# The second block of the channel mixer: all seven-product sets, behind the first down product

## The chip, the cores and the metric

The kernel runs on one NeuronCore of a Trainium2 chip. The metric is the device time of one execution in microseconds. The time before is a median of 2115.37 us over three runs (2115.2 to 2117.08).

## The reference, cut to what matters

Two layers of a diffusion backbone on 640 tokens (512 latent and 128 context tokens). Each layer mixes tokens (retention and neighbourhood attention), adds the result to the residual, and ends with a channel mixer. The change lies in the channel mixer alone:

```python
D_MODEL = 1024; DEPTH = 2
D_FF = -(-8 * D_MODEL // (3 * 256)) * 256          # 2816

def swiglu(h, wg, wu, wd):
    return (jax.nn.silu(h @ wg) * (h @ wu)) @ wd

def block_tail(...):
    ...
    x = x + g1[:, None, :] * rmsnorm(mixed, n_post_mix)
    hf = modulate(rmsnorm(x, n_pre_ffn), sh2, sc2)
    return x + g2[:, None, :] * rmsnorm(swiglu(hf, w_ffn_gate, w_ffn_up, w_ffn_down), n_post_ffn)
```

## The kernel before, in words

**Numbers as two halves.** Every fp32 operand of a matmul is split into a high part (a copy to fp32r by ScalarE) and a low part (the difference, by VectorE). A product is three matmuls: high by high, high by low, low by high (`product`, L502 to L504; `linear`, L514 to L517). Weights come in slabs of 128x1024 fp32, 512 KB each, from `w_main` into the buffers `raw`; `wh` and `wl` hold their halves (ScalarE's and VectorE's `split`). SP issues the slabs in the order in which `main_slabs` lays them, each as soon as the last user of its buffer is done. The modulated tokens stand feature by feature in `hmh` and `hml` (8 chunks of 128 features, 640 tokens).

**The blocks.** The 2816 hidden features are 11 blocks of 256 (`FB`). A block needs two gate columns and two up columns of 128 features each, then silu(gate) times up gives its hidden activations (`hidh`, `hidl`), and its down product adds to the output of five token tiles (`down`, tiles of 128 tokens, 12 matmuls of 128x512 per tile).

**Plain columns.** A column is 8 chunks x 3 matmuls x 2 halves of 320 tokens, 48 matmuls of 128x320, in one of two PSUM buffers `unit`. Block 0 is all plain columns: `first_columns` computes three of them (up to two wait for the last token tile), and a `column` the fourth. Its second hidden column is gated on VectorE (L2298) once that fourth column is there, copied on ScalarE (L1599), and its low part taken on VectorE (`hid_ready`).

**Seven products.** A pair of columns (256x1024 weights by 1024x640 activations, taken as a 2x2 by a 2x2) is also computed with seven products instead of eight (`seven`; each product is 4 chunks x 3 = 12 matmuls of 128x320). That needs sums of the tokens, once per layer (`t1` to `t4`: `sum_of_tokens`, `last_sum_of_tokens`, low parts in `low_of_tokens`), and sums of the weights, once per pair (`pair_sums`: four operations of 128x512 into `e0w` or `e1w` and back into `raw`; then the halves of the two slabs and of the sums in three parts, `pair_high` on ScalarE, `pair_low` on VectorE). The products go round four PSUM banks (`place`). VectorE adds each to the others (`seven_add`, L2344), and TensorE waits for those additions (`seven_added`) before it writes a bank again: the sixth product waits for the first addition, the seventh for the second.

**The order around the change.** With `SEVEN = 2`, blocks 2 to 10 are sets of seven throughout, while block 1 is mixed: its two gate columns are plain and come right behind block 0's, then the down product of block 0, then one set of seven for block 1's up columns (`seven(0)`). So a layer has `SEVENS = 19` sets. From there on TensorE alternates two sets of seven for block b and the down product of block b-1. VectorE's order is written out by hand in `first_block`, `second_block` and `seven_block`, ScalarE's under the same names. GpSimd issues DMAs alone in this stretch (the copies of the tokens to `x_keep`, L1194).

## Time and profile before

| | |
|---|---|
| median of the runs | 2115.37 us |
| the profiled execution | 2116.27 us, its span on the core 2114.5 us |
| TensorE busy | 2092.1 us (99%), 13850 matmuls |
| VectorE busy | 1558.5 us (74%) |
| ScalarE busy | 937.1 us (44%) |
| GpSimd busy | 101.6 us (5%) |
| granted TensorE clock | 1.00 |

Busy time is the time in which an engine executes something. A matmul's row is longer than its share of the engine's time, as matmuls are pipelined: what one costs is the distance from its start to the next start. On VectorE and ScalarE too a row overlaps the next one by about 0.1 us. Times are microseconds from the span's start, and the idle time in brackets behind a row is the engine's wait just ahead of it and what ended it.

### The profile page before, as it was taken

To read this page: it belongs to the slowest core of one execution; us is meant where nothing else is said; L and a number is where in the kernel's file an instruction comes from. 1 tells how busy PE (TensorE), PEld (TensorE's weight loads), DVE (VectorE), ACT (ScalarE), POOL (GpSimd) and SP (SyncE) were. 2 spreads that over 40 slices of the span, in tenths; PEclk is the share of its full clock that TensorE was granted. 3 is DMA by queue.
4 is the path that set the end of the run, shared out by engine and by line. 5 is a ranking of instruction groups with operands and counts; after the bars stand their busy time and mean duration, and the time that the engine had idled before them with its cause. 6 is when DMAs were issued, how large, how long until landed. Compare 5 with 4: busy or idle time off the path is not lost.

```text
span 2114.5 us, 33751 instructions
## 1 busy us (share of the span) xinstructions
PE 2092.1 (99%) x13850; PEld 1993.0 (94%) x13850; DVE 1558.5 (74%) x2493; ACT 937.1 (44%) x1490; POOL 101.6 (5%) x195
## 2 busy tenths in 40 slices
PE   8999999999999999999999999999999999999998
PEld 6999999899989999999899999999999899999997
DVE  6688767777757887887877776755854688787786
ACT  6555432476335432333485554235743553233333
POOL 0000001110000000000000000011100000000000
PEclk9999999999999999999999999999999999999999
DMA  8333355324333222222433333532233312222223
GB/s 317 110 120 122 103 174 176 138 93 148 102 131 119 80 80 80 80 80 88 162 132 120 115 109 131 169 127 79 86 120 130 130 61 80 80 80 82 97 82 139
DMA packets 63241, 246.05 MB, mean 116 GB/s; under 512 B 7792, under 2 KB 8080, under 8 KB 60400
## 3 DMA queue, kind: packets, MB, share of 16 engines
q1 hardware_dynamic: 42480, 158.55, 21.6%
q0 software_dynamic: 20608, 85.35, 11.6%
q8 instruction: 110, 1.80, 0.3%
q14 instruction: 43, 0.35, 0.1%
HBM read 230.20 MB, written 13.66 MB: 115 GB/s over the span
## 4 chain that ended last, share of the span: by engine, by line
PE 93%; DVE 3%; ACT 2%; DMA 1%; issue 0%; DVEq 0%; POOL 0%; POOLq 0%
PE unit L502 11%; PE unit L503 11%; PE unit L504 11%; PE unit L514 10%; PE unit L517 10%; PE unit L515 10%; PE sc L502 4%; PE sc L503 4%; PE sc L504 4%; PE tp L502 4%; PE tp L503 4%; PE tp L504 4%; PE tp L862 1%; PE sc L838 1%; PE unit L889 1%; PE unit L888 1%
## 5 line engine op out<-in xcount | busy, mean ns | idle before, releaser
L1773 DVE TENSOR_TENSOR wl<-raw,wh 128x1024 fp32r<-128x1024 f32 x200 | 242.2, 1221 | 119.3 <-ACT wh L1224 117.3
L514 PE MATMUL unit<-hmh,wh 128*128 128x320 f32 x1056 | 318.5, 309 | 1.8 <-DVE vl L1783 1.5
L515 PE MATMUL unit<-hml,wh 128*128 128x320 f32 x1056 | 318.1, 309 | 0.0
L1224 ACT ACTIVATE wh<-raw 128x1024 fp32r<-128x1024 f32 x200 | 206.0, 1050 | 99.6 <-DMA raw<-w_main 99.5
L517 PE MATMUL unit<-hmh,wl 128*128 128x320 f32 x1056 | 240.6, 309 | 0.0
L1872 DVE CUSTOM_DVE_ANT_0 junk<-ada,csb,par 128x1024 f32<-128x1024 f32 x160 | 205.6, 1285 | 29.3 <-DMA ada<-w_ada 9.7
L514 PEld LDWEIGHTS unit<-hmh,wh 128*128 128x128 f32 x1056 | 198.3, 188 | 2.4 <-issue 2.4
L515 PEld LDWEIGHTS unit<-hml,wh 128*128 128x128 f32 x1056 | 198.3, 188 | 0.0
L502 PE MATMUL unit<-wh,hmh 128*128 128x256 f32 (+1 forms) x544 | 178.8, 329 | 0.3 <-DVE wl L1773 0.3
L503 PE MATMUL unit<-wl,hmh 128*128 128x256 f32 (+1 forms) x544 | 177.7, 327 | 0.0
L504 PE MATMUL unit<-wh,hml 128*128 128x256 f32 (+1 forms) x544 | 177.7, 327 | 0.0
L517 PEld LDWEIGHTS unit<-hmh,wl 128*128 128x128 f32 x1056 | 176.6, 188 | 0.0
L502 PE MATMUL unit<-wh,hidh 128*128 128x512 f32 x440 | 171.6, 390 | 0.0
L503 PE MATMUL unit<-wl,hidh 128*128 128x512 f32 x440 | 171.4, 390 | 0.0
L504 PE MATMUL unit<-wh,hidl 128*128 128x512 f32 x440 | 171.2, 389 | 0.0
L502 PE MATMUL unit<-hmh,wh 128*128 128x320 f32 (+2 forms) x384 | 123.5, 322 | 0.5 <-DVE hml L1783 0.5
L504 PE MATMUL unit<-hmh,wl 128*128 128x320 f32 (+2 forms) x384 | 118.7, 309 | 0.0
L503 PE MATMUL unit<-hml,wh 128*128 128x320 f32 (+2 forms) x384 | 118.6, 309 | 0.0
L502 PEld LDWEIGHTS unit<-wh,hmh 128*128 128x128 f32 x544 | 104.3, 192 | 9.1 <-issue 0.5
L504 PEld LDWEIGHTS unit<-wh,hml 128*128 128x128 f32 x544 | 104.3, 192 | 8.8
L503 PEld LDWEIGHTS unit<-wl,hmh 128*128 128x128 f32 x544 | 104.3, 192 | 8.5
L1620 ACT ACTIVATE wh<-raw 128x1024 fp32r<-128x1024 f32 x38 | 40.2, 1057 | 149.2 <-DVE e0w L2321 147.7
(472 smaller groups left out, 5431.6 us busy)
## 6 DMA issues: line engine op xcount, KB each, us to landing
raw<-w_main SPq DMA_DIRECT2D x276, 512.0 KB, 3.8
ada<-w_ada POOLq DMA_DIRECT2D x80, 512.0 KB, 4.5
first<-w_first SPq DMA_DIRECT2D x8, 1024.0 KB, 19.2
x<-x_keep POOLq DMA_DIRECT2D x3, 2560.0 KB, 11.1
bias<-biases POOLq DMA_DIRECT2D x32, 192.0 KB, 2.7
x_keep<-x POOLq DMA_DIRECT2D x10, 512.0 KB, 2.9
bias<-biases POOLq DMA_DIRECT2D x16, 256.0 KB, 4.1
gains<-g_rows POOLq DMA_DIRECT2D x4, 1024.0 KB, 6.1
```

The source lines that it names most:

```text
L502: pe.matmul(out, a[0], b[0], start=first, stop=False)
L503: pe.matmul(out, a[0], b[1], start=False, stop=False)
L504: return pe.matmul(out, a[1], b[0], start=False, stop=last)
L514: pe.matmul(u[:, h, 0:n], a[0], xs[h][0], start=f, stop=False)
L515: pe.matmul(u[:, h, 0:n], a[0], xs[h][1], start=False, stop=False)
L517: mm = pe.matmul(u[:, h, 0:n], a[1], xs[h][0], start=False, stop=z)
L838: pe.matmul(sc[hh][:, 0:n], (nqh, nql)[a][rows[hh], j * P:(j + 1) * P], (nkh, nkl)[b][rows[hh], first * P:first * P + n], start=t == 0, st ...
L862: mm = pe.transpose(tp[hh][:, to * P:(to + 1) * P], s[:, hh, n * P:(n + 1) * P], ident[:, :])
L1224: act.activation(wh[slot[i]][:, :], raw[slot[i]][:, :], ACT.Copy).then_inc(w_hi[slot[i]], 1)
L1620: act.activation(wh[slot[i + 1]][:, :], raw[slot[i + 1]][:, :], ACT.Copy).then_inc(w_hi[slot[i + 1]], 1)
L1773: dve.tensor_tensor(wl[slot[i]][:, :], raw[slot[i]][:, :], f32(wh[slot[i]][:, :]), ALU.subtract)\
L1872: a = dve.tensor_tensor_reduce(junk[:, :], ada[ada_slot[i]][:, :], csb[:, which, :], 1.0, par[:, l, B_ADA + chunk:B_ADA + chunk + 1], ALU. ...
```

## The change

All of block 1 becomes sets of seven (`SEVEN = 1`, 20 sets a layer), and they move behind the first down product, which now follows the fourth column at once. That down product takes its first two tiles chunk by chunk: the first half of both tiles waits for the first hidden column alone, the second half for the second. GpSimd computes the weight sums of block 1's two pairs. The slabs are laid in the new order. VectorE and ScalarE do block 0's and block 1's steps in a new hand-written order, and the sums of the third pair (block 2's gate columns) come inside the second set's additions.

```diff
-SEVEN, SIX = 2, 6
-SEVENS = 2 * (FB - SEVEN) + 1
+SEVEN, SIX = 1, 6
+SEVENS = 2 * (FB - SEVEN)
...
                 def down(b):
+                    weights = [slab(512)[1:] for _ in range(2)]
+                    units = []
+                    for k in range(2 if b == 0 else 0):
+                        pe.wait_ge(hid_ready, downs.value() * 2 + k + 1)
+                        for t in range(2):
+                            if k == 0:
+                                units.append(U.take())
+                                U.add()
+                            mm = down_part(units[t], b, t, k, weights, k == 0, k == 1)
+                            if k == 1:
+                                mm.then_inc(unit_ready, 1)
                     pe.wait_ge(hid_ready, downs.value(1) * 2)
-                    weights = [slab(512)[1:] for _ in range(2)]
-                    for t in range(TILES):
+                    for t in range(2 if b == 0 else 0, TILES):
                         u = U.take()
                         U.give(down_tile(u, b, t, weights, True, True))
...
                     pe.wait_ge(w_lo[slot[i + 1]], turn_of[i + 1])
-                    pe.wait_ge(ts_ready, 4 * l + 4)
+                    pe.wait_ge(ts_ready, 4 * l + 3)
                     pe.wait_ge(seven_copied, r + 1)
                     quarters(4, s3, t3_)
                     pe.wait_ge(seven_added, 7 * r + 1)
                     quarters(5, a12, b21)
                     pe.wait_ge(seven_added, 7 * r + 2)
+                    pe.wait_ge(ts_ready, 4 * l + 4)
                     quarters(6, a22, t4_)
...
                 first_columns(2 * l)
                 column()
-                column()
-                column()
                 down(0)
-                seven(0)
-                for b in range(SEVEN, FB - 1):
+                gate_up(1)
+                for b in range(2, FB - 1):
                     gate_up(b)
                     down(b - 1)
...
                 g.wait_ge(hm_ready, (2 * l + 1) * 2 * TILES)
                 if l == 0:
                     g.wait_ge(ada_done, FIRST_ADA)
+                for r in range(2):
+                    i = l * PER_LAYER + W_O + KD + 6 + 2 * r
+                    for n in range(2):
+                        g.wait_ge(w_in[slot[i + n]], turn_of[i + n] * 16)
+                    (a11, a12), (a21, a22) = ([raw[slot[i + n]][:, h * 512:h * 512 + 512] for h in range(2)] for n in range(2))
+                    s1, s2_, s4 = (wwhole[r][:, n, :] for n in range(3))
+                    g.tensor_tensor(s1, a21, a22, ALU.add)
+                    g.tensor_tensor(a21, a11, a21, ALU.subtract)
+                    g.drain()
+                    g.tensor_tensor(s2_, s1, a11, ALU.subtract)
+                    g.drain()
+                    g.tensor_tensor(s4, a12, s2_, ALU.subtract).then_inc(ws_full, 1)
...
+                def first_block():
+
+                    u = U.get()
+                    for of, part in whole(u, sig[:, :], True):
+                        a = act.activation(part, of, ACT.Silu)
+                    U.release(a)
+                    U.add()
+                    U.wait_released(1)
+                    act.activation(hidh[:, 0, 0, :], sig[:, :], ACT.Copy).then_inc(hid_hi, 1)
                     hids.add()
+                    split(2)
+
+                    act.wait_ge(bank_ready, 2 * l + 2)
+                    act.wait_ge(hid_ready, hids.count)
+                    act.activation(sig[:, 0:CUT], sc[0][:, 0:CUT], ACT.Silu)
+                    act.activation(sig[:, CUT:T], sc[1][:, 0:T - CUT], ACT.Silu).then_inc(bank_free, 1)
                     token_sums((0,))
+                    for part in range(3):
+                        pair_high(0, part)
+                    U.add()
+                    U.wait_released(1)
+                    act.activation(hidh[:, 0, 1, :], sig[:, :], ACT.Copy).then_inc(hid_hi, 1)
+                    hids.add()
                     for t in range(TILES):
                         u = U.get()
                         U.release(act.activation(mix[:, t, :], flat(u[:, :, :]), ACT.Copy))
+                        if t in (0, 2):
+                            token_sums((t + 1,))
...
+                U.add()
+                sum_of_tokens(0)
+                gated(0)
+                split(2)
+                pair_low(0, 0)
+                gated(1)
+                sum_of_tokens(1)
+                pair_low(0, 1)
+                sum_of_tokens(2)
+                low_of_tokens((0, 1))
+                pair_low(0, 2)
+                last_sum_of_tokens()
+                low_of_tokens((2, 3))
+                U.add(TILES)
                 for b in range(SEVEN, FB):
...
-    parts += [gate_up[0], gate_up[1][0::2], down[0], gate_up[1][1::2]]
-    for b in range(SEVEN, FB - 1):
+    parts += [gate_up[0], down[0], gate_up[1]]
+    for b in range(2, FB - 1):
         parts += [gate_up[b], down[b - 1]]
```

`gated(n)` is block 0's multiplication, its wait for ScalarE's copy, and the low part. In VectorE's `seven_block` of block 1, two low parts of the second pair (`pair_low(1, 0)` and `pair_low(1, 1)`) stand ahead of the first addition, the third behind it.

Where the work moved, in the program's order of layer 0. On TensorE, at the start of the first down product, before (the last rows of block 1's second gate column, then the first row of the down product; `wh_60` and `wl_52` are its weights):

```order
L515 MATMUL unit<-hml,wh_61 128x320
L514 MATMUL unit<-hmh,wh_61 128x320
L515 MATMUL unit<-hml,wh_61 128x320
L517 MATMUL unit<-hmh,wl_53 128x320 x2
L502 MATMUL unit<-wh_60,hidh 128x512 [waits w_lo0,unit_free0,w_lo1,hid_ready]
```

The same place after the change (the last row of block 0's fourth column, then the first halves of two tiles, and the first row of the second half):

```order
L517 MATMUL unit<-hmh,wl_195 128x320 x2
L502 MATMUL unit<-wh_62,hidh 128x512 [waits hid_ready,unit_free0,w_lo2,w_lo3]
L503 MATMUL unit<-wl_54,hidh 128x512
L504 MATMUL unit<-wh_62,hidl 128x512
L502 MATMUL unit<-wh_61,hidh 128x512
L503 MATMUL unit<-wl_53,hidh 128x512
L504 MATMUL unit<-wh_61,hidl 128x512
L502 MATMUL unit<-wh_62,hidh 128x512 [waits unit_free1]
L503 MATMUL unit<-wl_54,hidh 128x512
L504 MATMUL unit<-wh_62,hidl 128x512
L502 MATMUL unit<-wh_61,hidh 128x512
L503 MATMUL unit<-wl_53,hidh 128x512
```

One matmul later the second `hid_ready` is waited for. The two gate columns no longer stand between block 0's fourth column and the down product.

On VectorE, from the low parts of the first two token sums (`t1l`, `t2l`) on, before:

```order
L1783 TENSOR_TENSOR t1l<-t1w,t1h 128x1280 [waits ts_hi]
L1783 TENSOR_TENSOR t2l<-t2w,t2h 128x1280 [waits ts_hi]
L2316 TENSOR_TENSOR e1w<-raw_190 128x512 [waits w_in5,w_in4]
L2317 TENSOR_TENSOR raw_190<-raw_187,raw_190 128x512
L2319 TENSOR_TENSOR e1w<-e1w,raw_187 128x512
L2321 TENSOR_TENSOR e1w<-raw_187,e1w 128x512
L2276 TENSOR_TENSOR hmh_w<-hmh 128x4x320 [waits unit_ready]
L2277 TENSOR_TENSOR hml_w<-hml 128x4x320
L2279 TENSOR_TENSOR hml_w<-hmh_w,hml_w 128x4x320
L1783 TENSOR_TENSOR wl_186<-raw_187,wh_188 128x1024 [waits w_hi4,ws_full]
L1783 TENSOR_TENSOR wl_189<-raw_190,wh_191 128x1024 [waits w_hi5,ws_full]
```

And after, up to the first addition (`u_220`):

```order
L1787 TENSOR_TENSOR t1l<-t1w,t1h 128x1280 [waits ts_hi]
L1787 TENSOR_TENSOR t2l<-t2w,t2h 128x1280 [waits ts_hi]
L1787 TENSOR_TENSOR e0l<-e0w,e0h 128x1536 [waits ws_hi]
L2280 TENSOR_TENSOR hmh_w<-hmh 128x4x320
L2281 TENSOR_TENSOR hml_w<-hml 128x4x320
L2283 TENSOR_TENSOR hml_w<-hmh_w,hml_w 128x4x320
L1787 TENSOR_TENSOR hml<-hml_w,hmh 128x4x320 [waits ts_hi]
L1787 TENSOR_TENSOR t4l<-t4w,t4h 128x1280 [waits ts_hi]
L1787 TENSOR_TENSOR wl_186<-raw_187,wh_188 128x1024 [waits w_hi4,ws_full]
L1787 TENSOR_TENSOR wl_189<-raw_190,wh_191 128x1024 [waits w_hi5,ws_full]
L2327 TENSOR_TENSOR u_220<-sc,c_218 128x320 [waits seven_done,seven_copied]
```

The four rows of weight sums are gone from VectorE; the halves of the second pair (`wl_186`, `wl_189`) stand ahead of the first addition.

On GpSimd, where only DMAs stood, now (`e0w` and `e1w` are the sums of the first and second pair; the last row is the next DMA):

```order
L1222 ISA
L1222 TENSOR_TENSOR e0w<-raw_55 128x512 [waits w_in1,ada_done,w_in0,hm_ready,x_saved]
L1223 TENSOR_TENSOR raw_55<-raw_56,raw_55 128x512
L1225 TENSOR_TENSOR e0w<-e0w,raw_56 128x512
L1227 TENSOR_TENSOR e0w<-raw_56,e0w 128x512
L1222 TENSOR_TENSOR e1w<-raw_190 128x512 [waits w_in5,w_in4]
L1223 TENSOR_TENSOR raw_190<-raw_187,raw_190 128x512
L1225 TENSOR_TENSOR e1w<-e1w,raw_187 128x512
L1227 TENSOR_TENSOR e1w<-raw_187,e1w 128x512
L1195 DMA gains<-g_rows 128x2048 [waits seven_done]
```

The eight operations stand behind the copies of the tokens to memory; layer 1 has the same eight without the ISA row.

## Rows read from the trace of the kernel before

**Rows 1.** The page's parts 1 and 4: busy time per engine, and the chain.

```profile
PE 2092.1 (99%) x13850; PEld 1993.0 (94%) x13850; DVE 1558.5 (74%) x2493; ACT 937.1 (44%) x1490; POOL 101.6 (5%) x195
...
PE 93%; DVE 3%; ACT 2%; DMA 1%; issue 0%; DVEq 0%; POOL 0%; POOLq 0%
```

**Rows 2.** Windows: columns in the first row; layer 0, then layer 1.

```profile
core 0: us, PE busy (x) PEld busy (x) DVE busy (x) ACT busy (x) POOL busy (x), PEclk, DMA share, GB/s
662.20:669.24 7.04, 7.04 (x50) 7.04 (x49) 3.03 (x3) 2.38 (x4) 0.00 (x0) 1.00 0.04 15
669.24:683.32 14.08, 14.08 (x98) 14.08 (x97) 12.61 (x11) 5.99 (x6) 0.00 (x0) 1.00 0.13 38
683.32:696.95 13.63, 13.63 (x63) 11.27 (x61) 13.41 (x13) 10.27 (x10) 0.00 (x0) 1.00 0.12 38
696.95:709.27 12.32, 12.32 (x86) 12.32 (x85) 8.55 (x12) 3.79 (x4) 0.00 (x0) 1.00 0.25 86
...
1710.30:1724.40 14.10, 14.10 (x99) 14.10 (x98) 12.63 (x11) 5.99 (x6) 0.00 (x0) 1.00 0.11 39
1724.40:1738.00 13.60, 13.60 (x62) 11.26 (x61) 13.38 (x13) 10.27 (x10) 0.00 (x0) 1.00 0.12 40
```

**Rows 3.** Timeline, TensorE: start, duration, engine, line, what (number).

```profile
669.24 0.31 PE L514 MATMUL unit<-hmh,wh 128*128 128x320 f32 x1
...
683.32 0.39 PE L502 MATMUL unit<-wh,hidh 128*128 128x512 f32 x1
...
696.95 0.30 PE L502 MATMUL sc<-hmh,wh 128*128 128x320 f32 x1
```

**Rows 4.** Timeline, VectorE, from the first token sum to the hidden activations.

```profile
653.28 1.23 DVE L1773 TENSOR_TENSOR wl<-raw,wh 128x1024 fp32r<-128x1024 f32 x1
654.42 1.48 DVE L2267 TENSOR_TENSOR t1w<-hmh 128x1280 f32<-128x1280 f32 x1
...
659.13 1.23 DVE L1773 TENSOR_TENSOR wl<-raw,wh 128x1024 fp32r<-128x1024 f32 x1
660.27 0.88 DVE L2298 TENSOR_TENSOR sig<-unit,sig 128x384 f32<-128x384 f32 x2
661.96 0.82 DVE L1783 TENSOR_TENSOR hidl<-sig,hidh 128x640 fp32r<-128x640 f32 x1 [0.80 <-ACT hidh L1599]
...
669.44 0.82 DVE L2298 TENSOR_TENSOR sig<-unit,sig 128x640 f32<-128x640 f32 x1 [3.60 <-PE unit L517]
671.07 0.82 DVE L1783 TENSOR_TENSOR hidl<-sig,hidh 128x640 fp32r<-128x640 f32 x1 [0.81 <-ACT hidh L1599]
```

**Rows 5.** Timeline, VectorE, from there to the first addition.

```profile
672.02 1.23 DVE L1773 TENSOR_TENSOR wl<-raw,wh 128x1024 fp32r<-128x1024 f32 x1
673.16 1.49 DVE L2267 TENSOR_TENSOR t2w<-hmh,t1w 128x1280 f32<-128x1280 f32 x1
...
676.31 1.49 DVE L2267 TENSOR_TENSOR t4w<-hmh,t2w 128x1280 f32<-128x1280 f32 x1
...
679.47 1.49 DVE L1783 TENSOR_TENSOR t1l<-t1w,t1h 128x1280 fp32r<-128x1280 f32 x1
...
682.27 0.69 DVE L2316 TENSOR_TENSOR e1w<-raw 128x512 f32<-128x512 f32 x1
...
685.01 1.49 DVE L2276 TENSOR_TENSOR hmh_w<-hmh 128x1280 f32<-128x1280 f32 x1
...
689.39 2.35 DVE L1783 TENSOR_TENSOR wl<-raw,wh 128x1024 fp32r<-128x1024 f32 x2
691.66 1.75 DVE L1783 TENSOR_TENSOR e1l<-e1w,e1h 128x1536 fp32r<-128x1536 f32 x1
693.33 1.49 DVE L1783 TENSOR_TENSOR t4l<-t4w,t4h 128x1280 fp32r<-128x1280 f32 x1
...
700.73 0.49 DVE L2344 TENSOR_TENSOR u<-sc,c 128x320 f32<-128x320 f32 x1 [1.78 <-PE sc L504]
```

**Rows 6.** Timeline, ScalarE: the hidden copy, weight copies, a token sum's copy.

```profile
670.30 0.74 ACT L1599 ACTIVATE hidh<-sig 128x640 fp32r<-128x640 f32 x1 [5.72 <-DVE sig L2298]
...
684.12 1.05 ACT L1617 ACTIVATE wh<-raw 128x1024 fp32r<-128x1024 f32 x1
685.13 1.06 ACT L1620 ACTIVATE wh<-raw 128x1024 fp32r<-128x1024 f32 x1
...
687.19 1.48 ACT L1623 ACTIVATE e1h<-e1w 128x1536 fp32r<-128x1536 f32 x1
...
689.91 1.27 ACT L1579 ACTIVATE hmh<-hml_w 128x1280 fp32r<-128x1280 f32 x1
```

**Rows 7.** Timeline, GpSimd: its last row in this stretch.

```profile
644.55 0.53 POOL L1194 DMA_DIRECT2D x_keep<-x  x1 [11.64 <-DVE x L1805]
```

More of the change, by code:

```diff
@@ L1621, in pair_high @@
                     else:
[L1622 to L1623 removed]
+                        act.activation(wsum[r % 2][0][:, :, :], wwhole[r % 2][:, :, :], ACT.Copy).then_inc(ws_hi, 1)
                         slabs.add(2)
@@ L1676, in seven_block @@
                     else:
-                        for part in (0, 1):
+                        for part in range(3 if b == SEVEN else 2):
                             pair_high(r + 2, part)
                     for n in range(2):
-                        high_of_hidden(b, n)
-                    if b < FB - 1:
+                        act.wait_ge(seven_up, l * SEVENS + r + n + 1)
+                        act.activation(hidh[:, b % 2, n, :], sigs[n][:, :], ACT.Copy).then_inc(hid_hi, 1)
+                        hids.add()
+                    if SEVEN < b < FB - 1:
                         pair_high(r + 2, 2)
                 first_block()
-                second_block()
                 for b in range(SEVEN, FB):
                     seven_block(b)
-                    if b < FB - 1:
+                    if SEVEN < b < FB - 1:
                         U.add(TILES)
@@ L2314, in pair_sums @@
                     (a11, a12), (a21, a22) = ([raw[slot[i + n]][:, h * 512:h * 512 + 512] for h in range(2)] for n in range(2))
-                    s1, s2_, s4 = (wwhole[(r + 1) % 2][:, n, :] for n in range(3))
+                    s1, s2_, s4 = (wwhole[r % 2][:, n, :] for n in range(3))
                     dve.tensor_tensor(s1, a21, a22, ALU.add)
@@ L2419, in _, with gated @@
-                second_block()
+                    dve.wait_ge(seven_gate, (l * SEVENS + r) // 2 + 1)
+                    dve.wait_ge(seven_added, 7 * (l * SEVENS + r) + 14)
+                    for n in range(2):
+                        dve.tensor_tensor(sigs[n][:, :], usum[:, n * T:n * T + T], sigs[n][:, :], ALU.mult).then_inc(seven_up, 1)
+                def gated(n):
+                    u = U.get()
+                    if n:
+                        dve.wait_ge(bank_free, 2 * l + 2)
+                    else:
+                        U.wait_released(1)
+                    for part, to in whole(u, sig[:, :], n == 0):
+                        a = dve.tensor_tensor(to, part, to, ALU.mult)
+                    U.release(a)
+                    hids.add()
+                    dve.wait_ge(hid_hi, hids.count)
+                    lo(hidl[:, 0, n, :], sig[:, :], hidh[:, 0, n, :]).then_inc(hid_ready, 1)
```

169 lines of the change are left out of this document (41 added, 128 removed).

## The prediction, with its working

> **What bounds the kernel now.** I read the page's busy table first: TensorE is busy for 2092.1 of 2114.5 us, VectorE for 1558.5, ScalarE for 937.1 and GpSimd for 101.6 [rows 1]. The chain that ended last is TensorE for 93%. So a change pays only if it takes matmuls out, and it costs whatever it makes TensorE wait. Then I read the stretches of the channel mixer's start, where the change lies [rows 2]. TensorE is busy in every microsecond of them, at a granted clock of 1.00, the higher of its levels (2.4 GHz), in layer 0 and in layer 1 alike: the fourth column of block 0 takes 7.04 us, the two gate columns of block 1 14.08, the first down product 13.63, the seven products 12.32. VectorE is busy for 12.61 of the 14.08 and for 13.41 of the 13.63 us there. It is not the bottleneck, but it has no room in exactly the two stretches that the change moves against each other. I take the stretches' limits from the first matmuls behind them: 669.24, 683.32 and 696.95 [rows 3].
>
> **The products.** In each layer two gate columns (14.08 us) become one more set of seven (12.32): -1.76, over two layers -3.5 us. The reordered first down product has the same 60 matmuls, 13.63/60 = 0.227 us each. This is all that the edit can give. About 0.2%, 4.2 us, is what a measurement of this kernel can tell from no change, so even the whole gain would read as no change.
>
> **The cover of block 0's hidden activations.** The down product now follows directly on the fourth column, so it would start at 669.24, 14.08 us earlier. Its second half needs the second hidden column. VectorE multiplies that column at 669.44, ScalarE copies it, and VectorE's low part ends at 671.07 + 0.82 = 671.89 [rows 4]. That is what the split of the first two tiles is for: 12 matmuls of the first half last to 669.24 + 12 x 0.227 = 671.97. The cover is 0.08 us, so I cost this wait at nothing while VectorE is punctual, and any lateness at that multiplication goes to TensorE whole.
>
> **VectorE's queue behind it.** Without waits TensorE ends the down product at 669.24 + 13.63 = 682.87 and takes 12.32/7 = 1.76 per product, so the fifth of the seven is due at 689.91, the sixth at 691.67. The sixth needs VectorE's first addition, and in the new order all of this stands between the hidden activations and that addition: two steps of the second token sum with drains, 676.31 - 673.16 = 3.15; a weight's low half, 1.13 (half of 691.66 - 689.39); two steps of the fourth sum, 679.47 - 676.31 = 3.16; the low parts of two sums, 682.27 - 679.47 = 2.80; the low part of the weight sums, 693.33 - 691.66 = 1.67; the last token sum, 689.39 - 685.01 = 4.38; a wait for ScalarE's copy of that sum, 1.27 [rows 5, 6]; two more low parts, 2.80; two low halves of the second pair, 2.27. That is 22.63 us, from 671.8 to 694.4; with the addition's 0.49 it ends at 694.9, 3.3 us after 691.67 (about 1.0 of it falls on the fifth product already, which needs the low part of the last sum, done near 690.9). Hand-overs of 0.03 to 0.1 us, as between the rows, make it 3.5. The seventh product waits for the second addition, which has another 1.67 us low part ahead of it: 694.4 + 0.40 + 1.67 + 0.49 = 697.0 against 694.9 + 1.76 = 696.7, so 0.3 more. I add 0.3 for block 2, whose pair sums and lows now stand between the second set's additions. Stalls 4.1 per layer; in the kernel before, the same work had the 14.08 us of gate columns to finish in, and VectorE there even waited 1.78 us for the first product [rows 5]. Neither layer's lost time can be made up, since TensorE has no idle time later. So without anything new from GpSimd: 2 x (-1.76 + 4.1) = +4.7 us.
>
> **GpSimd's sums.** VectorE loses eight additions and subtractions (2.7 us a pair: 682.27 to 685.01) [rows 5], which is already left out above. GpSimd does no arithmetic of this kind before the change: its rows here are DMA issues, the last at 644.55 [rows 7]. One operation of 128x512 is bounded below by VectorE's 0.69 for the same [rows 5], above by VectorE's 1.49 for 1280 elements; I take 1.05, ScalarE's time for 1024 elements [rows 6], as the operation has 2 x 512 elements to read. The Trainium skill's page GPSIMD Engine Reference, section 3.1, gives 4497 ns for 2048 elements, an estimate of 1.12 by a quarter of it; the sum below would be 1 us higher. No row here shows it.
> What such an operation does to VectorE is bounded by nothing (both run freely) and by its whole length (they take turns). I take turns: nearly all of VectorE's rows here read two operands from SBUF, as GpSimd's would, and nothing before shows that the paths are separate. The first four can start when the last low part of the modulated tokens is done, just as the row at 653.28 begins, and collide with the first token sum; the other four come when their slabs land, with the low halves ahead of the second multiplication. About seven of the eight lie before 669.44 in full. From 653.28 to there VectorE has 16.16 us, and work of 1.14 + 4.71 (three steps, 654.42 to 659.13) + 0.88 + 0.82 + 3 x 1.13 = 10.94 [rows 4]. It has 5.2 us of slack against 7 x 1.05 = 7.35, so the multiplication is 2.1 late, TensorE 2.0 a layer. Below 0.75 us an operation there is no loss; at 1.49 it is 5.1.
> The Trainium skill's page SBUF — State Buffer, section Who interferes with whom, says that a VectorE instruction with two SBUF inputs and a GpSimd one that reads SBUF lock each other out for a whole instruction. By that rule the sum is the one below; without it, it is the first rival's. No run here shows it yet.
> ScalarE has 1.05, 1.06 and 1.48 us of weight copies moved ahead of the second hidden copy; they fit into the 5.72 us that it waited there [rows 6], unless the sums are late. The slab loads on SP keep their places; the third pair now follows the down product, some 15 us before its sums.
>
> **Sum.** 2 x (-1.76 + 4.1 + 2.0) = +8.7 us. The profiled execution took 2116.27 us, 0.9 above the median of the runs shown, 2115.37. Hence 2125.0 against that execution, and 2124.0 for a median.
>
> **Rivals.** First, **GpSimd in nobody's way**: VectorE keeps its lengths, or its next instruction always goes first and GpSimd fits into the gaps (3.60 us before 669.44 alone [rows 4]). Then +4.7: 2120.1. For it speaks that nothing in the trace shows a collision; against it that the drains in the token sums let another engine in.
> Second, **a slow GpSimd**: at 1.49 an operation the stall before the down product is 5.1 instead of 2.0, 2130.2. The order also shows a new ISA row ahead of the first sum, issued after the DMA at 644.55 [rows 7]. It has 8 us until 653, and 13 until ScalarE wants the sums; if it takes more, each us is a us, once.
> Third, the other side: **VectorE comes in time**. It decides at one point: the first addition must end by 691.7, so the queue of 22.6 must be 19.3 or less. Then only the products count, -3.5: 2111.9, not slower. For it speaks that GpSimd takes 5.5 us off VectorE, and that before the change VectorE waited for TensorE at this very addition. Against it, that the stretch loses 14.08 us while the work relieved is 5.5, and that the rows stand almost without a gap from 672.02 on [rows 5].
>
> **Numbers.** Taking turns at about 1 us: 0.50, within 2121.7 to 2127. GpSimd in nobody's way: 0.30, within 2118.5 to 2121.5, three quarters of it over the bound of 2119.6. Slow GpSimd: 0.12. VectorE in time: 0.08, nearly all within 0.2%. Slower: 0.50 + 0.22 + 0.12 = 0.84; same 0.14; faster 0.02, as the products give less than the bound. The range leaves out the third rival and most of the second: 2118.2 to 2127.2.
>
> **What would show it.** The after trace should have TensorE stalls in each layer at three places: near the start or the second half of the first down product (0 if GpSimd is in nobody's way, 2 if they take turns), at the fifth and sixth products of the first set (1 and 2.4 us), and a fraction before the seventh. VectorE's three steps of the first token sum should end near 663 instead of 659 if they take turns, with gaps or lengths of GpSimd's size. If TensorE shows no idle time in the first set, the queue was counted wrong; if GpSimd's rows run beside unchanged VectorE rows, the turns were.

## The result, and the profile after

The changed kernel takes a median of 2129.2 us (four runs, 2128.87 to 2130.49) against 2115.55 for the kernel before, measured beside it (2115.2 to 2117.08). The ratio is 1.0065, with a 95% interval of 1.0053 to 1.0077: slower, by more than the 0.2% that a measurement tells apart. The profiled execution took 2128.91 us, its span 2127.1, 12.6 more than the 2114.5 of before. The forecast was 2124.0, with a range of 2118.2 to 2127.2: the sign held, the size lay beyond the range. Two executions of the kernels below took 3434 and 4171 us, far above the others of the same kernel, and their medians leave them out.

The page's busy table and chain, which answer to [rows 1]:

```profile
PE 2092.6 (98%) x13826; PEld 1989.4 (94%) x13826; DVE 1571.8 (74%) x2501; ACT 941.7 (44%) x1494; POOL 130.8 (6%) x211
...
PE 90%; DVE 4%; ACT 2%; issue 2%; DVEq 1%; DMA 1%; POOL 0%; POOLq 0%
```

GpSimd is busy for 29 us more. VectorE is busier too, by 13 us, though it does four operations a layer fewer on weight sums: two pairs went to GpSimd, and one of them is new with the twentieth set. On the chain VectorE and the issue of instructions took shares over from TensorE. The waits of TensorE (engine, line, what it waited for: us in total, times, longest) show where. None of these five stands among the waits of the kernel before:

```profile
PE sc L502 <- DVE u L2327: 4.1, 2, 2.0
PE unit L502 <- DVE sig L2382: 2.9, 2, 1.7
PE sc L502 <- issue: 2.6, 2, 1.3
PE unit L502 <- DVE hidl L1787: 1.7, 2, 0.8
PE unit L502 <- ACT mix L1656: 0.8, 2, 0.4
```

The windows from the first down product to the first set of seven, and from there to the second set, in layer 0 (they answer to [rows 2]; there the down product had 13.63 us and a set 12.32):

```profile
core 0: us, PE busy (x) PEld busy (x) DVE busy (x) ACT busy (x) POOL busy (x), PEclk, DMA share, GB/s
...
669.26:686.90 17.64, 14.63 (x63) 10.96 (x62) 16.24 (x11) 9.50 (x9) 6.59 (x5) 1.00 0.00 0
686.90:703.35 16.45, 13.09 (x86) 12.33 (x84) 14.78 (x15) 6.02 (x6) 0.00 (x0) 1.00 0.19 65
```

So the down product lost 17.64 - 13.63 = 4.0 us and the first set 16.45 - 12.32 = 4.1; 0.2 more follow at block 2. In layer 1 the same stretches run from 1716.93 to 1734.01 and to 1750.44: 3.4 and 4.1, and 0.2. With the 1.76 that each layer's products save, that is 16.1 - 3.5 = +12.6 us, the difference of the spans to the tenth. On balance nothing is lost or won elsewhere.

The matmuls in front of which TensorE stood, layer 0 (start, duration, engine, line, what, and the wait ahead of it):

```profile
672.54 0.50 PE L502 MATMUL unit<-wh,hidh 128*128 128x512 f32 x1 [1.74 <-DVE sig L2382]
...
675.05 0.50 PE L502 MATMUL unit<-wh,hidh 128*128 128x512 f32 x1 [0.85 <-DVE hidl L1787]
...
681.32 0.50 PE L502 MATMUL unit<-wh,hidh 128*128 128x512 f32 x1 [0.43 <-ACT mix L1656]
...
695.37 0.39 PE L502 MATMUL sc<-hmh,wh 128*128 128x320 f32 x1 [1.28 <-issue]
...
699.40 0.41 PE L502 MATMUL sc<-hmh,wh 128*128 128x320 f32 x1 [2.03 <-DVE u L2327]
```

The first three lie in the down product, the last two open the fifth and the sixth product. The seventh starts another 0.2 late, too little for a wait in brackets. GpSimd's rows tell what is behind the first three (the last row is layer 1's third operation):

```profile
653.33 2.35 POOL L1222 TENSOR_TENSOR e0w<-raw 128x512 f32<-128x512 f32 x1 [8.29 <-DVE hml L1787]
655.64 2.54 POOL L1223 TENSOR_TENSOR raw<-raw,raw 128x512 f32<-128x512 f32 x1
666.68 1.30 POOL L1225 TENSOR_TENSOR e0w<-e0w,raw 128x512 f32<-128x512 f32 x1 [8.50 <-issue]
668.12 1.30 POOL L1227 TENSOR_TENSOR e0w<-raw,e0w 128x512 f32<-128x512 f32 x1
669.37 1.30 POOL L1222 TENSOR_TENSOR e1w<-raw 128x512 f32<-128x512 f32 x1
670.63 2.25 POOL L1223 TENSOR_TENSOR raw<-raw,raw 128x512 f32<-128x512 f32 x1
673.03 1.29 POOL L1225 TENSOR_TENSOR e1w<-e1w,raw 128x512 f32<-128x512 f32 x1
674.46 1.68 POOL L1227 TENSOR_TENSOR e1w<-raw,e1w 128x512 f32<-128x512 f32 x1
...
1713.04 2.05 POOL L1225 TENSOR_TENSOR e0w<-e0w,raw 128x512 f32<-128x512 f32 x1 [7.19 <-issue]
```

Four of layer 0's eight take 1.30 us; the four that start while a row of VectorE with two SBUF inputs is under way take 1.7 to 2.5. Between the second and the third, where the first drain stands, 8.50 us pass in which GpSimd waits for nothing that the profile names (7.19 in layer 1). So the sums of the first pair are there at 669.4, just when the second multiplication is due. The new ISA row cost nothing that shows: the first sum starts at 653.33, right behind the low part that it waits for. VectorE's rows show both effects, the turns and the late sums:

```profile
654.44 2.58 DVE L2271 TENSOR_TENSOR t1w<-hmh 128x1280 f32<-128x1280 f32 x1
657.10 3.99 DVE L2269 TENSOR_TENSOR t1w<-t1w,hml 128x1280 f32<-128x1280 f32 x2
...
669.45 2.31 DVE L1787 TENSOR_TENSOR wl<-raw,wh 128x1024 fp32r<-128x1024 f32 x1 [3.19 <-POOL e0w L1227]
671.68 0.81 DVE L2382 TENSOR_TENSOR sig<-unit,sig 128x640 f32<-128x640 f32 x1
673.30 1.70 DVE L1787 TENSOR_TENSOR hidl<-sig,hidh 128x640 fp32r<-128x640 f32 x1 [0.81 <-ACT hidh L1652]
674.92 2.57 DVE L2271 TENSOR_TENSOR t2w<-hmh,t1w 128x1280 f32<-128x1280 f32 x1
...
698.86 0.49 DVE L2327 TENSOR_TENSOR u<-sc,c 128x320 f32<-128x320 f32 x1
```

The step of the first token sum that took 1.48 [rows 4] takes 2.58, and the first step of the second token sum 2.57 instead of 1.49 [rows 5]. The low half ahead of the second multiplication waits 3.19 us for GpSimd's sums and then takes 2.31 instead of 1.23; the multiplication starts at 671.68 instead of 669.44 [rows 4], the low part of the hidden activation takes 1.70 instead of 0.82 and ends at 675.0 instead of 671.89. The first addition starts at 698.86, 7.2 us after 691.67, when the prediction has the sixth product due.

### The profile page after: what moved, and what is told of

The parts are those of the page before. It is cut to its first block, busy times and chain, and to the rows that moved or that the text cites. A ratio compares the mean times of both kernels' runs of the same rounds, so it can differ in the third digit from the quotient of the medians.

```text
span 2127.1 us, 33792 instructions
## 1 busy us (share of the span) xinstructions
PE 2092.6 (98%) x13826; PEld 1989.4 (94%) x13826; DVE 1571.8 (74%) x2501; ACT 941.7 (44%) x1494; POOL 130.8 (6%) x211
## 4 chain that ended last, share of the span: by engine, by line
PE 90%; DVE 4%; ACT 2%; issue 2%; DVEq 1%; DMA 1%; POOL 0%; POOLq 0%
PE unit L502 11%; PE unit L503 11%; PE unit L504 11%; PE unit L514 9%; PE unit L517 9%; PE unit L515 9%; PE sc L502 4%; PE tp L502 4%; PE sc L503 4%; PE sc L504 4%; PE tp L503 4%; PE tp L504 4%; PE tp L862 1%; PE sc L838 1%; PE unit L889 1%
## 5 line engine op out<-in xcount | busy, mean ns | idle before, releaser
L1777 DVE TENSOR_TENSOR wl<-raw,wh 128x1024 fp32r<-128x1024 f32 x196 | 237.1, 1221 | 118.5 <-ACT wh L1253 117.0
L514 PE MATMUL unit<-hmh,wh 128*128 128x320 f32 x992 | 299.2, 309 | 1.3 <-DVE vl L1787 1.0
L515 PE MATMUL unit<-hml,wh 128*128 128x320 f32 x992 | 298.7, 309 | 0.0
L517 PE MATMUL unit<-hmh,wl 128*128 128x320 f32 x992 | 226.1, 309 | 0.0
L514 PEld LDWEIGHTS unit<-hmh,wh 128*128 128x128 f32 x992 | 186.2, 188 | 1.7 <-issue 1.7
L515 PEld LDWEIGHTS unit<-hml,wh 128*128 128x128 f32 x992 | 186.3, 188 | 0.0
L517 PEld LDWEIGHTS unit<-hmh,wl 128*128 128x128 f32 x992 | 165.8, 188 | 0.0
```

The lines of the kernel that those rows point to most:

```text
L514: pe.matmul(u[:, h, 0:n], a[0], xs[h][0], start=f, stop=False)
L515: pe.matmul(u[:, h, 0:n], a[0], xs[h][1], start=False, stop=False)
L517: mm = pe.matmul(u[:, h, 0:n], a[1], xs[h][0], start=False, stop=z)
L1777: dve.tensor_tensor(wl[slot[i]][:, :], raw[slot[i]][:, :], f32(wh[slot[i]][:, :]), ALU.subtract)\
```

## The experiments

All changes are to the changed kernel, and all of it is given per layer where nothing else is said. What a place loses is the time from start to start above the 13.63 and 12.32 us.

### Zeros in place of GpSimd's sums

```diff
-                    g.tensor_tensor(s1, a21, a22, ALU.add)
...
-                    g.tensor_tensor(s4, a12, s2_, ALU.subtract).then_inc(ws_full, 1)
+                    g.memset(wwhole[r][:, :, :], 0.0).then_inc(ws_full, 1)
```

> GpSimd's eight additions and subtractions a layer are left out; it writes zeros into the buffers of the weight sums instead (one row a pair, no operand read), so block 1's products are computed from wrong sums. After the change TensorE lost 8.3 us in layer 0 and 7.7 in layer 1 at the start of the mixer: 3.9 and 3.3 of them at the first down product, 4.3 at the fifth to seventh product and behind. Theory (GpSimd's operations make all of the stall at the down product, VectorE's queue makes the rest): the down product loses under 0.3, the fifth to seventh products still 4.2 to 4.4 a layer, 2 x (4.3 - 1.76) = +5.1 against the kernel before: 2120 to 2121. Rival (ScalarE's copies moved ahead of the second hidden activation, or the new order itself, make the first stall): 3 us a layer stay at the down product, 2126 to 2129.

The kernel leaves the sums out, so its products are not the right ones; only its time counts. Measured: 2122.09 us median, ratio 1.0031 (1.0017 to 1.0046). The down product loses 0.2 us in both layers, VectorE's first token sum takes 1.49 and 3.06 where the change had 2.58 and 3.99, and both waits at the products are still there, the fifth's shorter:

```profile
691.56 0.38 PE L502 MATMUL sc<-hmh,wh 128*128 128x320 f32 x1 [0.88 <-issue]
...
695.59 0.41 PE L502 MATMUL sc<-hmh,wh 128*128 128x320 f32 x1 [2.03 <-DVE u L2322]
```

So GpSimd's sums, with their drains, make all but 0.2 of the stall at the down product, and ScalarE's moved copies at most that. The median lies 1.1 us above the expected 2120 to 2121, the profiled execution (2123.45) 2.5. The windows of the same trace show why:

```profile
690.00:695.60 5.60, 2.69 (x18) 2.19 (x16) 5.60 (x6) 3.20 (x3) 0.00 (x0) 1.00 0.00 0
...
697.00:700.00 3.00, 3.00 (x13) 3.00 (x13) 2.29 (x6) 0.00 (x0) 0.00 (x0) 0.50 0.00 0
```

After the two stalls (1.04 and 2.19 us) the granted clock falls to 0.50, the lower level (1.2 GHz), for about 3 us. Matmuls of 128x320 then start 0.267 us apart instead of 0.147: 1.4 us a layer, in both layers. The first set loses 4.9 us, 1.4 of them so.

### Semaphores in place of GpSimd's drains, and a drain ahead of the sums

```diff
+        ws_part = sem("ws_part")
...
+                    done = 4 * l + 2 * r
                     g.tensor_tensor(s1, a21, a22, ALU.add)
-                    g.tensor_tensor(a21, a11, a21, ALU.subtract)
-                    g.drain()
-                    g.tensor_tensor(s2_, s1, a11, ALU.subtract)
-                    g.drain()
+                    g.tensor_tensor(a21, a11, a21, ALU.subtract).then_inc(ws_part, 1)
+                    g.wait_ge(ws_part, done + 1)
+                    g.tensor_tensor(s2_, s1, a11, ALU.subtract).then_inc(ws_part, 1)
+                    g.wait_ge(ws_part, done + 2)
```

> GpSimd's two drains a pair become waits on a semaphore that its own instructions raise. After the change its third operation starts 8.5 us after the second ended (7.2 in layer 1), with nothing named as the releaser. Theory (the drain is what takes the 8 us): the third operation follows within 0.5 us, the first pair's sums are there by 662, VectorE's low half before the second multiplication no longer waits (3.19 us after the change), and the stall at the down product falls to what taking turns costs, 0.5 to 2.5 us instead of 3.9: 2123 to 2127. Rival (the 8 us belong to something else, such as the operation itself or what GpSimd fetches): the third operation still starts near 666.7, 2129.

The second kernel keeps the drains and adds one:

```diff
                     g.dma_start(x_keep[:, t, :], x[:, t, :]).then_inc(x_saved, 16)
+                g.drain()
                 g.wait_ge(x_saved, (l * (TILES + 1) + TILES) * 16)
```

> One drain more on GpSimd, right behind its last DMA issue of the tokens (at 645 us), 8 us before its first addition. Theory (the first drain behind a row of DMA issues takes 7 to 8 us, whenever it comes): the added drain takes them where GpSimd waits anyhow, and the later one 0.2 us; the third operation starts by 659 and the time is that of the kernel with semaphores in place of drains. Rival 1 (the drain waits for the first two additions' own results, however late): the gap stays at 8.5 us, 2129. Rival 2 (each of two drains pays it): the first addition starts no later than before, the gap stays.

Measured: 2127.88 us (ratio 1.0060, 1.0044 to 1.0076) with semaphores and 2125.04 (1.0048, 1.0032 to 1.0063) with the added drain; their profiled executions differ by 1.5 us. The stalls are alike; in the first kernel's trace the granted clock fell to 0.50 in layer 1, which makes about 1.1 of the 1.5. The first's median lies 0.9 above its expected range, and the second's 2.8 below the first's, where both were expected to be the same. The gap is gone in both. GpSimd with the added drain:

```profile
655.25 2.54 POOL L1224 TENSOR_TENSOR raw<-raw,raw 128x512 f32<-128x512 f32 x1
657.93 2.35 POOL L1226 TENSOR_TENSOR e0w<-e0w,raw 128x512 f32<-128x512 f32 x1
660.43 2.37 POOL L1228 TENSOR_TENSOR e0w<-raw,e0w 128x512 f32<-128x512 f32 x1
662.85 1.30 POOL L1223 TENSOR_TENSOR e1w<-raw 128x512 f32<-128x512 f32 x1
```

The first pair's sums end at 662.8, the second pair's at 670.5. What is left at the down product is turns, on VectorE's rows of the same kernel:

```profile
654.05 2.58 DVE L2272 TENSOR_TENSOR t1w<-hmh 128x1280 f32<-128x1280 f32 x1
656.71 4.93 DVE L2270 TENSOR_TENSOR t1w<-t1w,hml 128x1280 f32<-128x1280 f32 x2
...
664.75 4.56 DVE L1778 TENSOR_TENSOR wl<-raw,wh 128x1024 fp32r<-128x1024 f32 x2
669.24 2.31 DVE L1788 TENSOR_TENSOR wl<-raw,wh 128x1024 fp32r<-128x1024 f32 x1
671.47 0.81 DVE L2383 TENSOR_TENSOR sig<-unit,sig 128x640 f32<-128x640 f32 x1
```

Against their lengths without GpSimd (1.49, 3.06, 2.35 and 1.23, as VectorE has them with the zeros) these rows grew by 6.3 us; with 0.5 at a low part between them that is 6.8 for eight operations, 0.85 each. The multiplication starts at 671.47, 2.0 late. TensorE loses 0.5 ahead of the down product, whose weights' low halves (the row of 4.56) end only at 669.31, and 2.1 in it, where the change lost 4.0.

### Three marks around the drain

```diff
+                g.memset(mark[:, :], 0.0)
+                g.drain()
+                g.memset(mark[:, :], 0.0)
+                g.drain()
+                g.memset(mark[:, :], 0.0)
                 g.wait_ge(x_saved, (l * (TILES + 1) + TILES) * 16)
```

> As the run with the added drain, but three writes of 128x8 zeros on GpSimd as time marks: one right behind its last DMA issue (at 645 us), a drain, the second, another drain, the third. Theory (the first drain behind DMA issues takes 7 to 8.5 us by itself, with no arithmetic ahead of it and whether the transfers have landed or not): the second mark comes 7 to 9 us after the first, the third within 0.3 us of the second. Rival 1 (the drain lasts until the transfers have landed, about 3 us after their issue): the second mark comes 2 to 4 us after the first. Rival 2 (the time belongs to the change from DMA issues to arithmetic, not to the drain): the first mark is late, near 652, and the drain behind it short. The kernel's time like that with the added drain, 2125.

Measured: 2128.03 us (three runs, 2125.88 to 2128.13; ratio 1.0057, 1.0034 to 1.0079). The median is 3 us above the expected 2125; the profiled execution, at 2125.88, has the stalls of the kernel with the added drain, and what the other two runs lost is open. The marks are plain (the last row is layer 1's second):

```profile
644.24 0.53 POOL L1211 DMA_DIRECT2D x_keep<-x  x1 [11.57 <-DVE x L1815]
644.76 0.12 POOL L1212 MEMSET mark<- 128x8 f32 x1
653.37 0.10 POOL L1214 MEMSET mark<- 128x8 f32 x1 [8.48 <-issue]
653.59 0.11 POOL L1216 MEMSET mark<- 128x8 f32 x1
...
1698.81 0.10 POOL L1214 MEMSET mark<- 128x8 f32 x1 [7.17 <-issue]
```

The first drain behind the DMA issues takes 8.48 us (7.17 in layer 1), the next one 0.1. It is the same whether it comes at once behind the issue or 13 us later, as in the change, when the transfers (2.9 us from issue to landing) had long landed: not the transfers' time, and not the arithmetic's. Whether the DMA issues make it, or the time since the last drain, no run separates.

### The sums' users behind the second multiplication

```diff
-                pair_low(0, 0)
                 gated(1)
+                pair_low(0, 0)
...
-                    for part in range(3):
-                        pair_high(0, part)
+                    pair_high(0, 0)
...
+                    pair_high(0, 1)
+                    pair_high(0, 2)
```

> VectorE takes the first low half of pair 0 behind the second hidden activation instead of ahead of it, and ScalarE the second slab's and the sums' high parts behind its copy of that activation; GpSimd is left as it is. Theory A (the down product's stall comes from engines that wait for late sums: VectorE 3.19, ScalarE 1.88 us): the second multiplication starts near 669.5 instead of 671.68, the stall at the down product falls from 3.9 to 1 to 2 (turns with GpSimd's operations that now lie there), the queue behind is 1.1 longer: 2 us less a layer at the one place, 1 more at the other, 2126 to 2128. Theory B (turns alone): the multiplication and the low part stay as late as GpSimd's four to six operations make them, the stall stays at 3 to 4 and the queue is longer: 2130 to 2132.

Measured: 2128.94 us, ratio 1.0066 (1.0050 to 1.0082): no gain, and between the ranges of both theories. VectorE multiplies on time (669.33, theory A), beside a GpSimd operation at 669.25 and without growing (0.82). But two places on, TensorE waits for ScalarE, whose copy of the second token sum stands ahead of its copy of the second output tile:

```profile
678.82 1.27 ACT L1608 ACTIVATE t2h<-t2w 128x1280 fp32r<-128x1280 f32 x1 [3.55 <-DVE t2w L2270]
...
681.05 0.50 PE L502 MATMUL unit<-wh,hidh 128*128 128x512 f32 x1 [2.66 <-ACT mix L1657]
...
699.12 0.41 PE L502 MATMUL sc<-hmh,wh 128*128 128x320 f32 x1 [2.04 <-DVE u L2328]
```

The down product loses 3.9 as before, and the sixth product starts at 699.12 against 699.40. The last row is the lesson: it waits for VectorE's first addition, and VectorE's rows between the multiplication and there wait for ScalarE alone, for no matmul. So what TensorE wins earlier it would lose again here, as long as that queue stays as it is; this is read from the order of the rows, since the down product's stall moved here and did not go away. In the profiled execution the clock fell after this wait too (1.2 us in the first set of either layer), so its times are no measure of the new order by itself.

### VectorE takes the sums itself

```diff
-                gated(0)
+                gated(0, lambda: pair_sums(0, last=False))
+                pair_sums(0, first=False)
                 split(2)
-                pair_low(0, 0)
-                gated(1)
+                pair_sums(1)
+                gated(1, lambda: pair_low(0, 0))
```

(The second argument runs between the multiplication and the wait for ScalarE's copy. GpSimd's eight operations are taken out; that part of the edit is not shown.)

> GpSimd's part alone is undone: VectorE takes the weight sums of both pairs itself, and takes them ahead of the second multiplication: two operations of pair 0 while it waits for ScalarE's copy of the first hidden activation, two behind the low part, pair 1's four behind the down weights; its low half of pair 0's first slab goes into the wait for ScalarE's second copy. Eight operations at 0.69 us, 5.5, against the 5.2 of slack that VectorE had there in the kernel before. Theory (GpSimd is a loss in itself, since one of its 1.30 us operations stops VectorE for 1.1 to 1.3, longer than VectorE needs for the same sum): the down product loses 0.2 to 0.7 us instead of 3.9, the queue behind stays, first addition near 695.5, total 4.3 to 4.7 a layer: 2120 to 2122. Rival (VectorE has no room for the sums, which is what the change gave GpSimd them for): the multiplication is 2 to 3 us late and the time is that of the change, 2127 to 2129.

Measured: 2123.19 us, ratio 1.0036 (1.0022 to 1.0049). The down product loses 0.46. The first set loses 4.9, of which 1.4 are matmuls at the lower clock, as with the zeros: that is more than the distance to the expectation, 1.2 us. VectorE takes all eight sums and is on time:

```profile
668.14 0.69 DVE L2295 TENSOR_TENSOR e1w<-raw,e1w 128x512 f32<-128x512 f32 x1
669.38 0.82 DVE L2373 TENSOR_TENSOR sig<-unit,sig 128x640 f32<-128x640 f32 x1 [0.54 <-PE unit L517]
```

So handing the sums to GpSimd cost 3 to 3.5 us a layer at the down product, where VectorE had room for them.

### The queue alone

```diff
-                    pe.wait_ge(ts_ready, 4 * l + 3)
+                    pe.wait_ge(ts_ready, 4 * l + 4)
...
                     for part in (0, 1):
-                        pair_low(r + 1, part)
+                        if b > SEVEN:
+                            pair_low(r + 1, part)
...
                         if g == 0:
-                            pair_low(r + 1, 2)
+                            pair_low(r + 1, 2 if b > SEVEN else 0)
...
                         seven_add(i, 2, u2, u4[:, :], 1)
+                        if g == 0 and b == SEVEN:
+                            pair_low(r + 1, 1)
...
+                        if g == 0 and b == SEVEN:
+                            pair_low(r + 1, 2)
                         seven_add(i, 4, u4, to[1][:, HALF:T])
...
-                low_of_tokens((2, 3))
+                low_of_tokens((3, 2))
```

(In block 1, `b == SEVEN`, the second pair's two low halves and the low part of its sums now stand behind the first, second and third addition.)

> GpSimd as in the change; of VectorE's queue alone the order is altered: pair 1's two low halves and its low part of the sums come behind the first, second and third addition instead of ahead of the first, and the fourth token sum's low part ahead of the third's, with TensorE's waits to match. Theory (the first addition's place in the queue sets when the sixth product starts, whatever happens before): two low halves, 2.36 us, go from ahead of the addition, so the sixth product starts near 697.0 instead of 699.40 and the seventh waits no more: 2.4 to 2.6 a layer, 2124 to 2125. Rival (the lows are only put off, and the second set's first products wait for them): under half of that, 2126.5 to 2129.

Measured: 2123.08 us, ratio 1.0036 (1.0023 to 1.0050). The down product loses what it did (4.0 and 3.4), the first set 1.5 instead of 4.1. The first addition starts at 694.70, the sixth and seventh product wait for nothing. What stays is the fifth, which waits for the third token sum's low part, done at 694.8:

```profile
694.88 0.38 PE L502 MATMUL sc<-hmh,wh 128*128 128x320 f32 x1 [1.27 <-issue]
```

The median fell by 6.1 us, the two stretches account for 5.2. The rest is no gain of the edit: in the trace 0.5 us lie ahead of layer 0's down product, which starts at 668.76 instead of 669.26, and 0.5 between the two layers' mixers, in stretches that the edit leaves alone.

### Both repaired, with GpSimd's sums and without

With them: the added drain, the short queue, the sums' users behind the multiplication, as above, and ScalarE's copy of the second token sum behind the second tile's copy:

```diff
-                        if t in (0, 2):
-                            token_sums((t + 1,))
+                        if t in (1, 2):
+                            token_sums((2 * t - 1,))
```

> GpSimd's added drain at 645 us, the low half of pair 0 and ScalarE's two copies behind the second hidden activation, ScalarE's copy of the second token sum behind the second tile's copy, and the shortened queue, all together: the best order with GpSimd's sums kept. From the rows of the runs before: multiplication at 669.3, low part at 671.0 to 671.5, then 23.6 us to the first addition with the added drain, less 2.36, plus 1.2: 22.4, the sixth product near 693.9 where 691.7 is due. Theory (losses of one engine after another add up to one delay of VectorE's queue): 2.2 to 2.8 lost a layer, 2116 to 2119. Rival (turns with GpSimd's last operations fall on the low part or the second sum and shift everything): 3.5 to 4.5 a layer, 2119.5 to 2122.

Measured: 2118.53 us, ratio 1.0014 (1.0005 to 1.0023). The down product starts 0.5 late and loses 0.2, the fifth product waits once more:

```profile
692.11 0.38 PE L502 MATMUL sc<-hmh,wh 128*128 128x320 f32 x1 [1.64 <-issue]
```

Without them, from the kernel in which VectorE takes the sums (the third argument of `pair_low` steps two slabs back; ScalarE's copies of the token sums, not shown, follow the new order):

```diff
                 gated(1, lambda: pair_low(0, 0))
                 sum_of_tokens(1)
-                pair_low(0, 1)
-                sum_of_tokens(2)
+                dve.tensor_tensor(whole_sums[3], h21, whole_sums[1], ALU.subtract)
                 low_of_tokens((0, 1))
                 pair_low(0, 2)
                 last_sum_of_tokens()
-                low_of_tokens((2, 3))
+                pair_low(0, 1, 2)
+                low_of_tokens((2,))
+                dve.tensor_tensor(whole_sums[3], whole_sums[3], l21, ALU.add).then_inc(ts_full, 1)
...
+                            seven_add(i, 2, u2, u4[:, :], 1)
+                            low_of_tokens((3,))
+                            seven_add(i, 3, u4, to[0][:, HALF:T], 2)
+                            pair_low(r + 1, 0)
+                            seven_add(i, 4, u4, to[1][:, HALF:T])
+                            pair_low(r + 1, 2)
```

> No sums on GpSimd: both pairs' sums on VectorE ahead of the second multiplication as in the run with VectorE's sums, and behind it the queue in order of need: second token sum, one step of the fourth, low parts of the first two, low part of the weight sums, the last token sum, a low half, low part of the third, the fourth sum's other step, two additions, the fourth's low part, then additions and pair 1's lows in turn. Until the first addition that is 3.0 + 1.5 + 3.0 + 1.7 + 4.4 + 1.2 + 1.5 + 1.5 = 17.8 us from 672.3: 690.1, where the sixth product is due at 691.7. Theory (the queue is all that stands between the change and its products): no stall at the fifth to seventh product, 0.2 to 0.3 at the down product, 0.3 to 0.6 at the next block, 2 x (0.7 - 1.76) = -2: 2113 to 2114.5, the first kernel of this row below the one before, though by less than the 0.2% that a measurement tells. Rival (another wait turns up, on ScalarE's copies or the second set's lows): 1 to 2 us a layer more, 2115.5 to 2118.

Measured: 2113.55 us (eleven runs) against 2115.40, ratio 0.9991 with an interval of 0.9983 to 1.0000. By the bound of 0.2% that is no change, but in the trace the stalls are gone but for small ones. The down product and the first set, and two rows of VectorE:

```profile
668.67:682.77 14.10, 14.06 (x62) 11.11 (x61) 13.73 (x11) 6.02 (x6) 0.00 (x0) 1.00 0.00 0
682.77:695.09 12.32, 12.32 (x86) 12.31 (x84) 11.60 (x12) 7.17 (x7) 0.00 (x0) 1.00 0.26 86
```

```profile
689.12 0.48 DVE L2320 TENSOR_TENSOR u<-sc,c 128x320 f32<-128x320 f32 x1
...
690.54 1.49 DVE L1777 TENSOR_TENSOR t4l<-t4w,t4h 128x1280 fp32r<-128x1280 f32 x1 [0.34 <-ACT t4h L1596]
```

The first addition starts at 689.12 where the sixth product comes at 691.57, the fourth low part ends at 692.0 where the seventh comes at 693.33. The set takes its 12.32 us without a wait, the down product 0.47 more than its 13.63, block 2 another 0.2: 2 x (0.66 - 1.76) = -2.2. VectorE is busy for 11.60 of the 12.32 us. By the trace the products' gain is there, less 0.66 us a layer. The medians, 1.85 us apart, can't tell it from no change, as the prediction said of the whole gain.

## Why the prediction was right in sign and short in size

**The products, -1.76 a layer: right.** The spans of before and after differ by the stalls less just this.

**VectorE's queue, 4.1 a layer: right, the size partly by luck.** 4.1 in the first set and 0.2 at block 2, at the three places named. But this is not the queue alone. The first addition stood 27.2 us behind the multiplication, of which 2.0 are turns, and TensorE itself came late. Without GpSimd's sums (the run with zeros) the first set loses 4.9, of which 1.4 are matmuls at the lower clock, so the queue by itself 3.5, against 3.8 foretold for the set. The prediction's eight sums less for VectorE are right for the stretch ahead of the first addition; over a layer there are four less.

**The cover of block 0's activations: the count was wrong, the conclusion nearly right.** I let 12 matmuls of the first half run to 671.97. Only six can while the multiplication is out: the second tile needs the PSUM buffer that the fourth column holds until it is done, which is why the row at 672.54 names VectorE's `sig`. With a punctual multiplication (669.44 + 0.82) that buffer is free in time, and the wait costs little, 0.2 us with the zeros. That any lateness there goes to TensorE whole held.

**GpSimd's sums, 2.0 a layer: the mechanism right, the term mis-sized, and this is the step that failed.** It measured 4.0 and 3.4. The turns themselves came out near their price: with the gap removed the multiplication is 2.0 late, for 2.1 foretold, though by another split: an operation takes 1.30 us, not 1.05, and all eight then lie ahead of the multiplication, but each costs VectorE 0.85, not its length. TensorE loses 2.6 and 2.5 us there instead of 2.0, since the low halves of the down weights come late too. The sentence that failed is "about seven of the eight lie before 669.44 in full". Four did in layer 0, and so the three steps of the first token sum ended at 661.1, not near 663 as foretold. The sentence counted GpSimd's operations and put its drains at nothing. The first drain behind DMA issues takes 8.5 and 7.2 us, so in layer 0 six of the eight came from 666.7 on: VectorE and ScalarE stood waiting for the sums ahead of the multiplication, and the later operations stretched the low part of the hidden activation and the second token sum. That the multiplication is 2.2 late in the change, close to the 2.1 foretold, is luck: 3.19 us of waiting for late sums stand where the prediction had turns. Against the run with the added drain the drain costs 1.4 and 0.9 us at the down product and 0.4 a layer at the first set, 3.1 together. The traces of all three kernels without the gap agree: over both layers TensorE loses 12.6 to 13.0 us in these places, the lower clock left out, where the change loses 16.1. Their medians, 2125.04, 2127.88 and 2128.03, lie 4.2, 1.3 and 1.2 us below the change's, so the size is read from the traces and not from the times. The range ended at 2127.2 because I gave GpSimd's part no more than the length of its operations; the rival of a slow GpSimd, 2130.2, has the time nearly right, by luck: its 1.49 us an operation is not what made it.

The sum with the measured terms is -3.5 + 8.6 + 7.5 = +12.6 us, the difference of the spans; the medians lie 13.65 apart, as the profiled execution of before lay 0.7 above its median and that of the change 0.3 below.

On turn-taking the Trainium skill's page SBUF — State Buffer, section Who interferes with whom, agrees with the traces in three points: rows with two SBUF inputs grow by 1.09 us beside a GpSimd operation of 1.30, a multiplication with one input from PSUM does not grow (0.82 at 669.33), and neither do VectorE's rows beside zeros that GpSimd only writes (1.22 and 1.49 beside the write at 653.65). The estimate of 1.12 us that I had worked out from a figure of the Trainium skill's page GPSIMD Engine Reference, section 3.1, is lower than the 1.30 measured here for 512 elements. The other rivals fell: GpSimd was in the way, and VectorE was not in time.

Not settled: what the drain waits for (no run looked inside it), and what the runs of the kernels with semaphores and with marks lost beyond their stalls.

## What to carry to other kernels

Work moved to an idle engine has to be priced by what it does to the engine it relieves: here each 1.30 us operation on GpSimd took 0.85 us from VectorE, which does the same in 0.69. Where one engine's queue sets a date that another engine has to keep, stalls of the other ahead of that date hide part of the queue's delay: here the first addition was 7.2 us late and cost 4.1, since TensorE was 4.0 late itself. Shortening the queue, in order of need, gained 6.1 us in the median, moving such a stall nothing. And count the drains and the waits of a moved sequence as instructions, with a price each.

## What the runs showed of the hardware

- A drain on GpSimd behind DMA issues took 8.48 and 7.17 us, the next one 0.1, with three marks around them; coming 13 us later it took the same (8.50 and 7.19). Put right behind the issues, where GpSimd waited anyhow, it left no gap later.
- A 128x512 addition or subtraction of fp32 takes 1.30 us on GpSimd and 0.69 on VectorE. Where VectorE's row had two SBUF inputs the two engines took turns: the row that came second grew, VectorE's rows from 1.49 to 2.58, GpSimd's from 1.30 to as much as 2.54.
- In four of the kernels' profiles the granted clock of TensorE went from 1.00 to 0.50 for about 3 us behind two stalls, of 1.0 to 1.4 and of 2.2 us with one product between them, and cost 1.2 to 1.4 us a layer. In the change's own profile, with like stalls (1.43 and 2.19), it stayed at 1.00 in both layers, as with the added drain (1.05 and 2.19); what decides it is open.
